# Triangular solves of the second half of each head pair: from POOL to VectorE, inside the next scan

## What is computed

```python
def gdn_chunk_scan(q, k, v, g, beta, s0):        # chunks of C = 64 tokens
    ...
    l_strict = jnp.where(strict, jnp.einsum('bnthd,bnshd->bnhts', k_beta, k) * decay, 0.0)
    eye = jnp.eye(C, dtype=jnp.float32)
    t_inv = lax.linalg.triangular_solve(eye + l_strict, jnp.broadcast_to(eye, l_strict.shape),
                                        left_side=True, lower=True, unit_diagonal=True)
    u = jnp.einsum('bnhts,bnshv->bnthv', t_inv, v_beta)
    w = jnp.einsum('bnhts,bnshd->bnthd', t_inv, k_beta * jnp.exp(g_cum)[..., None])
    ...
    def step(s, inp):
        w_n, u_n, qd_n, att_n, ke_n, d_n = inp
        v_new = u_n - jnp.einsum('bthd,bhdv->bthv', w_n, s)
        o_n = jnp.einsum('bthd,bhdv->bthv', qd_n, s) + jnp.einsum('bhts,bshv->bthv', att_n, v_new)
        s = s * d_n[..., None, None] + jnp.einsum('bshd,bshv->bhdv', ke_n, v_new)
        return s, o_n
```

## Time and profile before

| | |
|---|---|
| time, median of 3 runs | 2867.55 us (2862.31 to 2876.98) |
| profiled execution | 2868.03 us, of which 2866.2 us are the span of the profile |
| mean granted TensorE clock | 0.911 of full speed |
| busy: PE / PEld | 2496.9 us (87%) / 1726.3 us (60%) |
| busy: DVE / ACT / POOL | 1042.2 us (36%) / 755.9 us (26%) / 696.8 us (24%) |
| POOL, products L913 and differences L915 | 276.7 us and 296.5 us, 496 instructions each |
| chain that ended last | PE 21%, POOL 6%, issue 2%, DVE 2%, DMA 2%, ACT 1% of the span |

### The profile page before, as it was taken

How to read it: one execution, slowest core, us unless ns; L and a number is a source line. 1 busy time by engine, 2 the same in 40 slices (tenths; PEclk the granted TensorE clock), 3 DMA queues, 4 the chain that set the end, 5 groups by cost and what they waited for, 6 DMA issues and landing times. The chain is left out here.

```text
span 2866.2 us, 32126 instructions
## 1 busy us (share of the span) xinstructions
PE 2496.9 (87%) x11050; PEld 1726.3 (60%) x11050; DVE 1042.2 (36%) x2345; ACT 755.9 (26%) x1971; POOL 696.8 (24%) x1149
## 2 busy tenths in 40 slices
PE   7999997788988797899999999999757975689998
PEld 6567655363646686655574446776454755566677
DVE  0123235646564212433322121224736563223321
ACT  1112033313132021444422112204413231233421
POOL 1000000877475500000000000000688677200000
PEclk7898798999999779999999999869879987899999
DMA  6210121212122121111112331113212221132333
GB/s 210 90 59 30 52 68 54 63 34 79 51 75 57 62 78 52 61 52 54 59 45 74 105 104 59 45 54 94 80 43 63 73 75 43 31 99 73 104 98 137
DMA packets 210250, 203.43 MB, mean 71 GB/s; under 512 B 30218, under 2 KB 203758, under 8 KB 209582
## 3 DMA queue, kind: packets, MB, share of 16 engines
q1 hardware_dynamic: 204910, 180.26, 20.5%
q0 software_dynamic: 5184, 21.12, 2.2%
HBM read 184.51 MB, written 16.85 MB: 70 GB/s over the span
## 5 line engine op out<-in xcount | busy, mean ns | idle before, releaser
L957 PE MATMUL bank<-hT,ring 128*128 128x512 f32 (+2 forms) x1824 | 714.8, 535 | 12.7 <-DVE hT L1609 7.1
L957 PE MATMUL bank<-WORK 128*128 128x128 f32 (+7 forms) x2896 | 508.5, 346 | 213.2 <-DVE WORK L1862 170.6
L957 PEld LDWEIGHTS bank<-WORK 128*128 128x128 f32 (+4 forms) x2896 | 370.5, 202 | 351.7 <-issue 318.8
L957 PEld LDWEIGHTS bank<-hT,ring 128*128 128x128 f32 (+1 forms) x1824 | 337.7, 192 | 301.8 <-issue 268.8
L957 PE MATMUL bank<-ring,hT 128*128 128x256 f32 (+3 forms) x2240 | 484.4, 373 | 32.6 <-DMA ring<-in_w_in_dram 17.1
L957 PEld LDWEIGHTS bank<-ring,hT 128*128 128x128 f32 x2240 | 404.2, 196 | 115.4 <-issue 45.0
L915 POOL TENSOR_TENSOR WORK<-WORK 32x31 f32<-32x31 f32 (+15 forms) x496 | 296.5, 598 | 38.9
L913 POOL TENSOR_TENSOR WORK<-WORK 32x31 f32<-32x31 f32 (+15 forms) x496 | 276.7, 558 | 38.9
L957 PE MATMUL bank<-yT,ring 128*128 128x512 f32 (+1 forms) x768 | 274.1, 491 | 0.0
L945 POOL DMA_DIRECT2D yT<-xs x2 | 1.1, 567 | 1011.6 <-PE bank L957 1011.6
L957 PEld LDWEIGHTS bank<-yT,ring 128*128 128x128 f32 x768 | 138.5, 191 | 85.3 <-issue 76.1
(11 more groups left out here) (183 smaller groups left out, 2299.9 us busy)
## 6 DMA issues: line engine op xcount, KB each, us to landing
ring<-in_w_in_dram SPq DMA_DIRECT2D x92, 1024.0 KB, 5.4
ring<-in_ada_w_dram SPq DMA_DIRECT2D x24, 1024.0 KB, 5.3
ring<-in_w_branch_dram SPq DMA_DIRECT2D x24, 1024.0 KB, 5.3
LD<-WORK SPq DMA_DIRECT2D x64, 128.0 KB, 2.0
WORK<-XD POOLq DMA_DIRECT2D x64, 128.0 KB, 2.7
ring<-in_w_out_dram SPq DMA_DIRECT2D x8, 1024.0 KB, 5.3
ring<-in_mla_q_up_dram SPq DMA_DIRECT2D x8, 576.0 KB, 4.6
xs<-yT POOLq DMA_DIRECT2D x2, 2048.0 KB, 10.1
```

What stands on the lines that cost most here:

```text
L957: return nc.tensor.matmul(o, a, b, start=start, stop=stop, skip_group_check=True)
```

## The change

In `head`, only the half p = 0 keeps its solve. The solve of p = 1 becomes an item `sol2` of DVE. It stands in the plan after the first scan of the next part with the same pair (between `scan(l, g, 0)` and `scan(l, g, 1)` for g = 1, 2 and 3), and for g = 0 at the end of the list that precedes the eight parts. What POOL did after a solve (write to `XD`, wait, bring back) becomes an item `xd` of its own behind each `sol` and `sol2`; it stays on POOL, and waits for the engine that solved. The DVE instructions are the same list as POOL's, with the same waits. SP waits for `sol2` on DVE before it loads the blocks of the next p = 1 half.

```diff
@@ head, gdn
-        return weave(one, two) + [("db", l, g, p), ("sol", l, g, p)]
+        return weave(one, two) + [("db", l, g, p)] + ([("sol", l, g, p), ("xd", l, g, p)] if p == 0 else [])
+
+    def solve(l, g):
+        return [("sol2", l, g, 1), ("xd", l, g, 1)]
...
-        first += head(l, 0, 0) + head(l, 0, 1)
+        first += head(l, 0, 0) + head(l, 0, 1) + solve(l, 0)
...
-            body = invert(l, g, p) + scan(l, g, 2 * p) + scan(l, g, 2 * p + 1)
+            body = (invert(l, g, p) + scan(l, g, 2 * p) + (solve(l, g) if k in (2, 4, 6) else [])
+                    + scan(l, g, 2 * p + 1))
@@ SP
-                        sp.wait_ge(*done(("sol", (rounds(l, g) - 1) // 4, (rounds(l, g) - 1) % 4, p), "pool"))
+                        sp.wait_ge(*done((("sol", "sol2")[p], (rounds(l, g) - 1) // 4, (rounds(l, g) - 1) % 4, p), ("pool", "dve")[p]))
@@ POOL
-                    pool.wait_ge(*done(it, "pool"))
+                elif k == "xd":
+                    _, l, g, p = it
+                    n = rounds(l, g)
+                    rows = slice(32 * p, 32 * p + 32)
+                    y = SLY[rows, :].rearrange("q (i j) -> q i j", i=BASE)
+                    pool.wait_ge(*done((("sol", "sol2")[p],) + it[1:], ("pool", "dve")[p]))
@@ DVE
+                elif k == "sol2":
+                    _, l, g, p = it
+                    n = rounds(l, g)
...
+                    dve.wait_ge(s_lblk[p], 32 * (n + 1))
+                    if n or p:
+                        dve.wait_ge(s_xout, 16 * (2 * n + p))
+                    V_.tensor_tensor(a, a, bc(SLB[rows, :], 2, [BASE, BASE, BASE]), ALU.mult)
+                    link(dve, "dve", V_.memset(SLY[rows, :], 0.0))
+                    link(dve, "dve", V_.tensor_copy(SLY[rows, 0:BASE * BASE:BASE + 1], SLB[rows, :]))
+                    for j in range(BASE - 1):
+                        m, w = BASE - 1 - j, j + 1
+                        t = SLT[rows, 0:m * w].rearrange("q (i c) -> q i c", i=m)
+                        link(dve, "dve", V_.tensor_tensor(t, a[:, j + 1:BASE, j:j + 1].broadcast_to([BASE, m, w]),
+                                                              y[:, j:j + 1, 0:w].broadcast_to([BASE, m, w]), ALU.mult))
+                        ins = V_.tensor_tensor(y[:, j + 1:BASE, 0:w], y[:, j + 1:BASE, 0:w], t, ALU.subtract)
+                        if j < BASE - 2:
+                            link(dve, "dve", ins)
```

More of the change, by code:

```diff
@@ L313 @@
 NBANK = {"nh": 0, "cv": 0, "dsilu": 0, "dsil2": 0, "dnq": 0, "z2": 0, "rstd": 0, "gw": 2, "ge": 2, "mkv": 1,
-         "dt": 0, "db": 0, "sol": 0, "dv": 0, "dg": 2}
+         "dt": 0, "db": 0, "sol": 0, "sol2": 0, "xd": 0, "dv": 0, "dg": 2}
 READERS = {"xin": ("act",), "par": ("act",), "mod": ("dve",), "norm": ("act",), "z": ("act", "dve"),
@@ L642, in hybrid_block @@
         NOACT = {"nh", "cv", "pc", "mt", "mod", "out", "yT", "gatt", "gw", "mo", "d2", "ab",
-                 "dt", "db", "sol", "dv", "dx", "dya", "dyb", "sk", "sq", "su", "sa"}
+                 "dt", "db", "sol", "sol2", "xd", "dv", "dx", "dya", "dyb", "sk", "sq", "su", "sa"}
         NODVE = {"norm", "dqkv", "pc", "dnq", "xin", "gqk", "gv", "lr", "mp", "xout", "mkT",
-                 "db", "sol", "dx6", "dy6", "st"}
+                 "db", "sol", "xd", "dx6", "dy6", "st"}
         POOLK = {"sol"}
@@ L649, in hybrid_block @@
                 continue
-            if k not in ("nh", "cv", "dsilu", "dsil2", "dnq", "z2", "rstd", "dt", "db", "sol", "dv"):
+            if k not in ("nh", "cv", "dsilu", "dsil2", "dnq", "z2", "rstd", "dt", "db", "sol", "sol2", "xd", "dv"):
                 parts["pe"].add(k)
@@ L1857, in _ @@
                                                bc(pair(ERV, tt, g, r), 2, [P, 2, P]), ALU.mult)
+                elif k == "sol2":
+                    _, l, g, p = it
+                    n = rounds(l, g)
+                    rows = slice(32 * p, 32 * p + 32)
+                    a = SLA[rows, :].rearrange("q (i j) -> q i j", i=BASE)
+                    y = SLY[rows, :].rearrange("q (i j) -> q i j", i=BASE)
+                    dve.wait_ge(s_lblk[p], 32 * (n + 1))
[12 more added lines that the diff above has]
+                            link(dve, "dve", ins)
                 elif k == "dv":
```

## The result

The changed kernel takes 3071.26 us (median of 4 runs, 3066.72 to 3076.39) against 2870.24 us of the kernel before (4 runs beside it). The ratio is 1.0702, 95% interval 1.0667 to 1.0737: slower by 7.0%. The profiled execution took 3066.72 us, its span is 3064.9 against 2866.2, and the mean granted clock fell from 0.911 to 0.881.

What follows compares the result with a forecast made beforehand. TensorE (87% busy) and its order bound the kernel. Layer 0: 49 + 57.2 + 13 - 5 = 114; layer 1: 36 + 57.2 + 8 - 12 = 89; together +203 on 2868.0 gave 3070 us, range 3015 to 3130.

Steps and rivals of the forecast that it cites:

- signs: PE standing 20 us or more at six middle places, released by DVE; layer 0 dv(0,1) near 656, dv(1,1) near 821.
- What bounds the kernel: Whole kernel: TensorE, busy 87%, gains only where it stands; faster p=1 solves could give at most 50.5 us.
- Part 1: Length of one p=1 solve on DVE: 27 us, between 24 and 39.9.
- Rival (a): Solves on DVE: short rows are dear, 33.5 us a solve, 52 more, kernel 3122 us; chance 0.15.
- Part 2: Solves in mid-scan: nothing hides them, 28.6 us each at g=1 and g=2; +13 and +8 at g=3.
- The clock: After PE's standstill, clock 0.50 for 5 us, then 0.83: +2 us a solve at g=1 and g=2.
- old wait for x(3,1): PE's wait before dv(3,1), 12.92 us in layer 0, 20.55 in layer 1; takes part of the g=3 solve.
- Part 3: Solve of g=0: DVE waits for POOL's write, then solves, holding dproj(1): +49 us in layer 0, +36 in layer 1.
- Part 4: Relief at dproj(2) and dproj(3), where POOL and DVE no longer work together: -5 layer 0, -12 layer 1.
- At no cost: Split `xd`, SP's wait for `sol2` and POOL's p=0 solves of g=1 to 3: no cost.
- The point from which it turns: Solve length on DVE at which the sum turns: 27 - 203/8, near 2 us.
- Rival (c): Solves run in DVE's idle time; 50.5 us of waits and 17 us of relief are won: 2800 us, chance 0.03.

Runs made afterwards that it cites:

- no steps: Changed kernel with the 31 steps of each solve on DVE left out; opening product, memset and diagonal stay: 2890.83 us, ratio 1.0082.
- steps twice: Changed kernel with memset, diagonal and steps of each solve on DVE executed twice: 3260.16 us, ratio 1.1373.
- steps woven: Changed kernel with each p = 1 solve cut into 31 items woven among other work, waiting only for its own half: 2926.18 us, ratio 1.0202.

## Why the prediction held, step by step

The forecast of 3070 met 3071.26. The mechanism was the one that was forecast, and the runs bear it out; that it is off by only 1 us is luck, since steps were off in both directions and cancelled. Of its signs, PE stood over 20 us at five of the six middle places (17.05 at the sixth), but the profile names no releaser there, where I had said DVE (that it is DVE's solve shows in the order of times above, and in the runs without and with twice the steps); and dv(0,1) and dv(1,1) came at 667.77 and 829.87, 12 and 9 us later than told.

**What bounds the kernel, and the place of the loss.** Right. PE's order, not DVE's busy share, decides; no steps, steps twice and steps woven show it from three sides.

**Part 1, the solve.** I took 27 us between 24 and 39.9; all eight DVE solves took 25.3 (550.59 to 575.86, 787.07 to 812.35). The sum of 25.9, before I went up to 27 for the short rows, was the better value. What the short rows cost can be read where the same number of elements comes in few long rows and in many short ones. Timeline of DVE, the solve at 550.59: 31 rows of one word and 30 of two near its begin, two of 30 words near its end (one of 31 is the last difference above, 0.18 us):

```profile
553.36 0.20 DVE L1884 TENSOR_TENSOR WORK<-WORK 32x31 f32<-32x31 f32 x1
...
553.84 0.21 DVE L1884 TENSOR_TENSOR WORK<-WORK 32x60 f32<-32x60 f32 x1
...
575.19 0.21 DVE L1884 TENSOR_TENSOR WORK<-WORK 32x60 f32<-32x60 f32 x1
```

Rows of one word cost 0.02 us more than one row of 31, rows of two words nothing. The Trainium skill (Vector Engine (DVE) Microarchitecture Reference, SBUF access granule) asks for two adjacent words for the full rate, and the rows agree with that as far as 0.02 us can tell. What I weighed against the sum, all elements at the slower rate, was a misreading of where it applies: one step in 31 has rows of one word. Rival (a), with 33.5 us a solve, came true only for a solve beside POOL's (37.1), which the change doesn't have.

**Part 2.** I took 28.6 for each solve at g = 1 and g = 2; the four took 29.0, 25.4, 25.9 and 26.4, mean 26.7. The solve explains 1.7 of the 1.9 difference; why (1,1) of layer 0 is 3 us above the others is not traced. The clock did what the row of before had shown, and for a little longer. Windows of the changed kernel (us, busy PE, PEld, DVE, ACT, POOL, clock) around the standstill that ends at 813.58:

```profile
790.00:795.00 5.00, 0.00 (x0) 0.00 (x0) 4.45 (x17) 0.00 (x0) 0.00 (x0) 0.81 0.00 0
795.00:800.00 5.00, 0.00 (x0) 0.00 (x0) 4.62 (x12) 0.00 (x0) 0.00 (x0) 0.50 0.00 0
...
810.00:815.00 5.00, 1.42 (x7) 1.45 (x7) 4.69 (x18) 0.00 (x0) 0.80 (x1) 0.50 0.12 26
815.00:820.00 5.00, 4.27 (x20) 4.00 (x20) 1.23 (x5) 0.60 (x1) 2.82 (x4) 0.50 0.38 107
820.00:825.00 5.00, 5.00 (x34) 4.04 (x34) 3.03 (x11) 0.63 (x1) 0.00 (x0) 0.96 0.02 3
```

PE works some 6.5 us at the lower level (0.50, that is 1.2 GHz) after standing. At g = 3 I gave +13 and +8, it was +15.6 and +5.2. The old wait for x(3,1) is gone in layer 0, as told; in layer 1, 1.45 us of it are left (its dv at 2663.36). I have not traced the 3 us by which each is off.

**Part 3.** +49 and +36 were +52.9 and +36.8. Within it: POOL's solve with DVE standing took 39.8 us (39.9), its write landed 2.9 after (2.8), DVE stood 36.9 and 39.3 us, the solve took 1.7 less, and dv(0,0) came 53.7 us after DVE was free in layer 0 where I had 49. The missing 4.7: I counted 43 products of the projections and no others, but 8 records of the norms' products with the ones (four times 1.0 us, and 0.65 of waiting for the first and the last) lie between them, 5.5 us in all. The first 20 records after the standstill took 11.2 us (granted clock 0.79 in the mean from 576.6 to 588) where the next 20 took 8.75 (1.00 from 588 to 598), so the low clock cost 2.5 rather than 1. From PE's last product to dv(0,0) it was 9.0 us where I had 10.4. Timeline of PE, from the end of the standstill:

```profile
576.61 11.24 PE L966 MATMUL bank<-hT,ring 128*128 128x512 f32 x20 [52.47 <-DVE yT L1660]
588.50 1.10 PE L966 MATMUL bank<-RS,ONES 128*128 128x512 f32 x2 [0.65 <-ACT RS L1479]
589.43 8.75 PE L966 MATMUL bank<-hT,ring 128*128 128x512 f32 x20
...
616.92 3.60 PE L966 MATMUL bank<-hT,ring 128*128 128x512 f32 x8
```

The first row also shows that the last `yT` held PE, as said, for 52.5 us.

**Part 4.** The relief was -5 and -12; it was -9.5 (5.95 + 3.5) and -13.3 at (1,0) and (2,0), and 3.5 more at (3,0) in layer 1, where I had none. The taps went from 828 to 729 ns in the mean of all 192, which mixes two sizes; the 160 of 128x512 went from 880 to 753. The 0.70 us for a tap alone was a little low: 16 taps of 128x512 with POOL idle (2217 to 2262 us) took 750 ns in the mean. The pieces (1,0) and (2,0) of layer 0 shortened by 5.95 and 3.5 where I had 2.5 each; what in them did is not traced.

**At no cost.** The split `xd` costs nothing that can be told, as its own run shows. What I overlooked: two more items in the first list change where `weave` puts the others. The first solve of layer 0 starts 7.8 us later, 6.9 of them by the list. In the sum this was hidden by solves cheaper than I thought (8 x 1.7 = 14) and by a relief of 26 us rather than 17.

**The point from which it turns.** I said near 2 us a solve. Without the steps it is 2.5 us and the kernel 25 us slower; by the slope of one, a solve of no length would still be 5 us behind or, within the interval, even. A length at which this placement wins was not found. The 2 us rested on 27 for the solve and so were too high by the same 1.7.

**Rival (c)** was wrong for this placement but right about the resource: the waits for x(3,1), 33.5 us in the two layers, were to be had. The kernels with the last half alone on DVE are 28 and 36 us faster than before, with DVE's steps in DVE's waits instead of ahead of what PE needs.

## What to carry to other kernels

An engine that is busy 36% of the time has idle time in places, not everywhere; moving work to it pays only where the plan puts the pieces into the waits themselves, so look up the wait first and cut the work to fit it. The test is cheap: leave the moved work out, then do it twice, and a slope of one says that nothing hides it. When items are added to a list that is merged evenly, compare where the unrelated items land before blaming the new work, and count from a mark inside the same stage, since the stage itself began up to 10 us earlier or later from trace to trace.

## What the runs showed of the hardware

- The same list of 65 instructions on 32 partitions takes 25.3 us on VectorE while GpSimd is idle and 39.8 on GpSimd while VectorE stands (1.57 times). Nearly side by side VectorE takes 37.1 and GpSimd 42.5: VectorE pays 47%, GpSimd 7%. The taps show it too: 958 ns beside a solve of POOL, 750 with POOL idle.
- VectorE takes rows of two words as quickly as rows of 30 (60 elements, 0.21 us), and rows of one word 0.02 us slower than one of 31 (0.20 and 0.18).
- In the changed kernel TensorE stood 25.55 us; its granted clock fell to 0.50 (the 1.2 GHz level) while it stood, was still 0.50 from 813.58 to 820, when it worked again, and 0.96 in the 5 us behind.
